# A diagonal of inverse roots in the place of scaled rows, at the norms of a three-layer network

## The chip, the cores and the metric

The kernel runs on one core of a Trainium2 chip. The metric is the device time of one execution in microseconds. The core has five engines that run beside each other, each in its own order, and that wait for one another by semaphores: TensorE (PE; the weight loads of its products are shown as PEld), VectorE (DVE), ScalarE (ACT), GpSimd (POOL) and SyncE (SP), which here issues the loads from memory.

## The reference

256 rows of 1024 f32 numbers go through two layers, each a mixer and an expert feed-forward part, and then through a third block with pooling and attention. Ahead of each of the five parts stands a norm over the rows, and a sixth stands at the end:

```python
def rmsnorm(x, g):
    xf = x.astype(jnp.float32)
    y = xf * lax.rsqrt(jnp.mean(xf * xf, axis=-1, keepdims=True) + RMS_EPS)
    return y.astype(x.dtype) * g

for layer in range(DEPTH):                      # two layers
    x = x + mixer(x, *mixer_params[layer])      # norms 0 and 2
    x = x + peer_ffn(x, *ffn_params[layer])     # norms 1 and 3
...
h = _rmsnorm(x, norm_gain[l])                   # norm 4, ahead of the third block
...
return _rmsnorm(x, final_gain)                  # norm 5
```

Each normed matrix goes into a product with weights at once (`xn @ w_in`, `xi @ w_query`, `h @ w_in[l]`). For such a product the columns of the matrix must lie across the partitions, so it has to be turned.

## The kernel before

`X` holds the 256 rows as two halves of 128 partitions (index `t` or `tt`), each with 1024 f32. Weights come in 680 chunks of 128x1024 through four slots. Each chunk is split on the chip into a high part (`high`, ScalarE, L157) and a low part (`low_v` on VectorE, L162, or `low_g` on GpSimd, L167), and each product with them is three products, high by high, high by low and low by high (L174 to L176, or the two wide ones of L180 and L181). SyncE may load a chunk into a slot when the low part of the chunk four before it is made, and the high part of a chunk is made three chunks ahead of PE. `w_used` counts the chunks that PE is done with.

A norm `n` is spread over four engines, each of which runs its piece in its own order:

- `norm_scalar` (ScalarE): for each half of the rows, the squares of columns 0 to 511 and of 512 to 1023 with their sums (L253), in `SM` columns `2t` and `2t + 1`; then the root (L257) of what VectorE has put into column `4 + t`.
- `norm_sum` and `norm_vector` (VectorE): for each half of the rows, the sum of both columns (L262), the reciprocal of the root (L264), and the scaling of all 1024 columns into the arena tile `xs` (L270). On VectorE this stands behind the four additions to `X` of the part before (`out_add`, L240, ahead of norms 1, 3 and 5; `up_add`, L1261, ahead of norms 2 and 4).
- `norm_tensor` (PE): 8 blocks of 128x128 of each half are turned into the banks 0 to 3 (L285). At norms 1 to 4 idle products of the identity with itself (L275) stand ahead of them: 12 ahead of the first half's blocks and 4 ahead of the second's. Six more follow at the end of every norm. Their result is not used.
- `split_scalar` and `split_vector`: as soon as two blocks of the second half have been turned, ScalarE writes the high part of the turned columns with the gain (L296) and VectorE the low part (L304). PE's first real product of the next stage waits for the low parts of the first two of the eight column blocks (`wait_x`).

Norm 5 has no turning: VectorE multiplies `X` by the reciprocal root and the gain (L2271) and SyncE stores it.

The order on each engine is the order in which the code is written; no scheduler moves anything.

Of the kernel before, what the change touches and what calls it, by code (L numbers as in the profile page):

```python
# [7 lines left out]
ALU = mybir.AluOpType  # L8
ACT = mybir.ActivationFunctionType
# [12 lines left out]
EPS = 1e-6  # L22
# [49 lines left out]
def build(nc, d, out):  # L72
    ctx = ExitStack()
    with ctx:
        def sb(name, shape, dt=F32):
            return ctx.enter_context(nc.sbuf_tensor(name, shape, dt))

        def sem(name):
            return ctx.enter_context(nc.semaphore(name))

        X = sb("X", [128, 2, 1024])
# [24 lines left out]
        SM = sb("sm", [128, 128])  # L106
        PS = ctx.enter_context(nc.psum_tensor("ps", [128, 8, 512], F32))
        scr = nc.dram_tensor("scr_rel", [24, 512], F32, kind="Internal")
        ident = CST[:, C_ID:C_ID + 128]
# [17 lines left out]
        for beside in low_on_g:  # L127
# [8 lines left out]
        n_sq, n_ss, n_sd, n_xs, n_xT, n_xh, n_xl = (sem("norm_" + n) for n in (  # L136
            "squares", "sum", "root", "scaled", "turned", "high", "low"))
# [111 lines left out]
        def norm_scalar(a, n, xs, x_ready):  # L249
            for t in range(2):  # L250
                for h in range(2):
                    x_ready(t, h)
                    a.activation(xs[:, t, h * 512:h * 512 + 512], X[:, t, h * 512:h * 512 + 512], ACT.Square,  # L253
                                 accum_out=SM[:, 2 * t + h:2 * t + h + 1]).then_inc(n_sq, 1)
                a.wait_ge(n_ss, 2 * n + t + 1)
                v = SM[:, 4 + t:5 + t]
                a.activation(v, v, ACT.Sqrt, scale=1.0 / 1024, bias=SM[:, 127:128]).then_inc(n_sd, 1)  # L257

        def norm_sum(v, n, t):
            r = SM[:, 4 + t:5 + t]  # L260
            v.wait_ge(n_sq, 4 * n + 2 * t + 2)
            v.tensor_tensor(r, SM[:, 2 * t:2 * t + 1], SM[:, 2 * t + 1:2 * t + 2], ALU.add).then_inc(n_ss, 1)  # L262
            v.wait_ge(n_sd, 2 * n + t + 1)
            v.reciprocal(r, r).then_inc(vec.sem, vec.up())  # L264
            v.wait_ge(vec.sem, vec.n)

        def norm_vector(v, n, xs):
            for t in range(2):
                norm_sum(v, n, t)
                v.tensor_scalar(xs[:, t, :], X[:, t, :], SM[:, 4 + t:5 + t], None, ALU.mult).then_inc(n_xs, 1)  # L270

        def idle_products(t, bank, count):

            for _ in range(count):
                t.matmul(PS[:, bank, 384:512], ident, ident, start=True, stop=True)  # L275

        def norm_tensor(t, n, xs):
            for tt in range(2):
                if n:
                    idle_products(t, 6 if n % 2 else 3, (12, 4)[tt])  # L280
                t.wait_ge(n_xs, 2 * n + tt + 1)
                for kp in range(4):
                    for j in range(2):
                        k = 2 * kp + j
                        m = t.transpose(PS[:, kp, j * 256 + tt * 128:j * 256 + tt * 128 + 128],  # L285
                                        xs[:, tt, k * 128:k * 128 + 128], ident)
                    if tt == 1:
                        m.then_inc(n_xT, 1)
            idle_products(t, 7, 6)
# [119 lines left out]
        def mixer0_tensor(t):  # L409
            t.wait_ge(cst_in, 16)  # L410
            norm_tensor(t, 0, XS0)

            def q_bank(pair, j):
# [78 lines left out]
        def mixer0_scalar(a):  # L492
            a.wait_ge(eps_up, 1)
            table(a, ACT.Sqrt)
            norm_scalar(a, 0, XS0, lambda t, h: a.wait_ge(x_in[t], 16))
            high(a, 0)
            high(a, 1)
# [77 lines left out]
        def mixer0_vector(v):  # L575
# [5 lines left out]
            v.wait_ge(x_in[0], 16)  # L581
            v.wait_ge(x_in[1], 16)
            norm_vector(v, 0, XS0)
            low_v(v, 0)
            low_v(v, 1)
# [323 lines left out]
        def peer_tensor(t, l):  # L909
            wq, down, up = bases(l)  # L910
            n = 2 * l + 1
            norm_tensor(t, n, XS)

            for c in range(16):
# [123 lines left out]
        def peer_scalar(a, l):  # L1038
            wq, down, up = bases(l)
            n = 2 * l + 1  # L1040
            norm_scalar(a, n, XS, lambda t, h: x_after_out(a, 2 * l, t, h))
            split_scalar(a, n, (PV_FFN0, PV_FFN1)[l])
            for c in range(16):
# [219 lines left out]
        def peer_vector(v, l):  # L1263
            wq, down, up = bases(l)
            n = 2 * l + 1
            norm_vector(v, n, XS)
            split_vector(v, n, (PV_FFN0, PV_FFN1)[l])
            for c in range(16):
# [174 lines left out]

        def mixer1_tensor(t):
            norm_tensor(t, 2, XS)

            def nat_bank(nb, tt):
# [148 lines left out]

        def mixer1_scalar(a):
            norm_scalar(a, 2, XS, lambda t, h: x_after_up(a, 1, t, h))
            split_scalar(a, 2, PV_MIX1)

# [133 lines left out]

        def mixer1_vector(v):
            norm_vector(v, 2, XS)
            split_vector(v, 2, PV_MIX1)

# [432 lines left out]
        def block2_vector(v):  # L2171
# [31 lines left out]
            for c in range(24):  # L2203
# [13 lines left out]
                if c == 16:  # L2217
                    v.wait_ge(sw_up, 1)
                    for g in range(4):
                        m = v.scalar_tensor_tensor(out=MIX[:, g, :], in0=MIX[:, g, :], scalar=PVT[:, PV_PS + g:PV_PS + g + 1],  # L2220
                                                   in1=SAG[:, g, :], op0=ALU.mult, op1=ALU.mult)
# [43 lines left out]
                low_v(v, W0 + c + 2)  # L2265
            out_add(v, 4, W0 + 7, 10)
            for t in range(2):
                norm_sum(v, 5, t)
                if t == 0:
                    v.wait_ge(fg_in, 16)  # L2270
                v.scalar_tensor_tensor(out=X[:, t, :], in0=X[:, t, :], scalar=SM[:, 4 + t:5 + t], in1=FG, op0=ALU.mult,  # L2271
                                       op1=ALU.mult).then_inc(out_up, 1)
# [39 lines left out]
        @block.vector  # L2312
        def _(eng):
            mixer0_vector(eng)
            peer_vector(eng, 0)
            mixer1_vector(eng)
            peer_vector(eng, 1)
            block2_vector(eng)
# [108 lines left out]
```

## Time and profile before

| what | us |
|---|---|
| median of 3 runs | 2176.23 |
| lowest and highest | 2171.87, 2176.41 |
| the profiled execution | 2174.84 |
| its span in the profile | 2173.0 |
| PE busy | 2132.8 |
| VectorE busy | 1467.4 |
| ScalarE busy | 1278.1 |
| GpSimd busy | 349.4 |

The profile is one execution. Its span runs from the first to the last record; the time of the execution is 1.8 us more. Busy time is the sum of an engine's records. Matmuls are pipelined, so their durations overlap, and the pace of a row of them is read from their starts: where a row of the timeline stands for a merged group (`x8`), the start of the next row less its own start, divided by the count, is the time for one. "L285" is line 285 of the kernel. In brackets stands the time that the engine was idle ahead of the row and what ended it.

### The profile page before, as it was taken

What the parts mean: (1) busy time and instruction counts of PE and PEld (TensorE: products, weight loads), DVE (VectorE), ACT (ScalarE), POOL (GpSimd) and SP (SyncE); (2) the same over time, 40 slices, a digit from 0 to 9 for tenths busy, and PEclk for the clock granted to TensorE, in tenths of its full rate; (3) what the DMA queues carried; (4) which work ended last, traced back from release to release, by engine and by line L of the source; (5) the groups of instructions that cost most, each with busy time, mean ns of one, the idle gap of its engine ahead of it and who ended that gap; (6) DMA issues with size and microseconds to landing.
All of it is one profiled execution on the core that took longest, in us unless ns stands there. A gap on an engine that the chain in (4) does not pass through costs nothing.

```text
span 2173.0 us, 32843 instructions
## 1 busy us (share of the span) xinstructions
PE 2132.8 (98%) x12752; PEld 1860.5 (86%) x12752; DVE 1467.4 (68%) x2593; ACT 1278.1 (59%) x2172; POOL 349.4 (16%) x160
## 2 busy tenths in 40 slices
PE   8899999999999999997999999999999999999998
PEld 7789988888888888876899888888888888898997
DVE  7658988889855555557489888898555555423445
ACT  6655488877644444465545788776444444444454
POOL 1437800000000000001378000000000000243131
PEclk9999999999999999999999999999999999999999
DMA  6445655555566666642356555555666666754244
GB/s 219 146 133 165 183 172 171 169 167 172 174 196 193 194 193 194 194 165 91 117 165 185 168 172 174 166 167 163 203 193 193 194 193 194 258 184 146 78 136 126
DMA packets 104317, 373.19 MB, mean 172 GB/s; under 512 B 11564, under 2 KB 15044, under 8 KB 103780
## 3 DMA queue, kind: packets, MB, share of 16 engines
q1 hardware_dynamic: 104164, 371.11, 55.6%
q8 instruction: 101, 1.65, 0.3%
q14 instruction: 52, 0.43, 0.1%
HBM read 369.96 MB, written 1.10 MB: 171 GB/s over the span
## 4 chain that ended last, share of the span: by engine, by line
PE 91%; DVE 4%; ACT 2%; DMA 1%; issue 1%; POOL 0%; SPq 0%; ACTq 0%; DVEq 0%
PE ps L180 20%; PE ps L174 18%; PE ps L175 17%; PE ps L176 17%; PE ps L181 10%; PE ps L905 3%; PE ps L1950 1%; DVE WL L162 1%; PE ps L1928 1%; DMA raw<-in_w_qk_dram 1%; PE ps L275 1%; PE ps L884 1%; PE ps L1936 0%; DVE arena L1686 0%; PE ps L1410 0%
## 5 line engine op out<-in xcount | busy, mean ns | idle before, releaser
L157 ACT ACTIVATE WH<-raw 128x1024 fp32r<-128x1024 f32 x680 | 717.4, 1056 | 499.9 <-PE ps L176 450.9
L162 DVE TENSOR_TENSOR WL<-raw,WH 128x1024 fp32r<-128x1024 f32 x556 | 680.0, 1225 | 102.8 <-ACT WH L157 102.7
L180 PE MATMUL ps<-X,WH 128*128 128x512 f32 x1888 | 668.8, 398 | 0.1
L181 PE MATMUL ps<-X,WL 128*128 128x256 f32 x1888 | 527.9, 280 | 0.0
L167 POOL TENSOR_TENSOR WL<-raw,WH 128x1024 fp32r<-128x1024 f32 x124 | 307.7, 2484 | 1006.2 <-ACT WH L157 1005.3
L180 PEld LDWEIGHTS ps<-X,WH 128*128 128x128 f32 x1888 | 353.9, 187 | 78.9 <-issue 0.5
L174 PE MATMUL ps<-WH,X 128*128 128x512 f32 x960 | 379.7, 396 | 4.8 <-DVE X L733 1.6
L175 PE MATMUL ps<-WL,X 128*128 128x512 f32 x960 | 376.1, 392 | 0.0
L176 PE MATMUL ps<-WH,X 128*128 128x512 f32 x960 | 376.0, 392 | 0.0
L181 PEld LDWEIGHTS ps<-X,WL 128*128 128x128 f32 x1888 | 356.8, 189 | 0.0
L174 PE MATMUL ps<-X,WH 128*128 128x256 f32 x896 | 256.4, 286 | 0.8 <-DVE WL L162 0.6
L175 PE MATMUL ps<-X,WH 128*128 128x256 f32 x896 | 253.7, 283 | 0.0
L176 PE MATMUL ps<-X,WL 128*128 128x256 f32 x896 | 253.7, 283 | 0.0
L174 PEld LDWEIGHTS ps<-WH,X 128*128 128x128 f32 x960 | 181.9, 189 | 45.2 <-DVE X L1594 2.0
L176 PEld LDWEIGHTS ps<-WH,X 128*128 128x128 f32 x960 | 181.5, 189 | 38.3
L175 PEld LDWEIGHTS ps<-WL,X 128*128 128x128 f32 x960 | 181.8, 189 | 37.3 <-issue 0.5
L174 PEld LDWEIGHTS ps<-X,WH 128*128 128x128 f32 x896 | 171.9, 192 | 6.4 <-issue 3.0
L175 PEld LDWEIGHTS ps<-X,WH 128*128 128x128 f32 x896 | 172.0, 192 | 0.1
L176 PEld LDWEIGHTS ps<-X,WL 128*128 128x128 f32 x896 | 171.9, 192 | 0.0
L989 ACT ACTIVATE ONE<-ONE,GATE 128x128 f16<-128x128 f16 x512 | 167.6, 429 | 0.0
L1250 DVE TENSOR_TENSOR X<-arena,X 128x512 fp32r<-128x512 f32 x84 | 58.1, 692 | 161.9 <-ACT X L1036 161.9
L176 PE MATMUL ps<-WH,GL 128*128 128x512 f32 x352 | 137.0, 389 | 0.0
(295 smaller groups left out, 2367.6 us busy)
## 6 DMA issues: line engine op xcount, KB each, us to landing
raw<-in_l_down_dram SPq DMA_DIRECT2D x256, 512.0 KB, 3.6
raw<-in_l_up_dram SPq DMA_DIRECT2D x256, 512.0 KB, 4.2
raw<-in_l_wq_dram SPq DMA_DIRECT2D x32, 512.0 KB, 3.6
raw<-in_w_qk_dram SPq DMA_DIRECT2D x24, 512.0 KB, 3.9
raw<-in_w_gates_dram SPq DMA_DIRECT2D x24, 512.0 KB, 3.6
raw<-in_l_nat_dram SPq DMA_DIRECT2D x16, 512.0 KB, 3.5
raw<-in_l_wout_dram SPq DMA_DIRECT2D x16, 512.0 KB, 3.6
raw<-in_l_win_dram SPq DMA_DIRECT2D x16, 512.0 KB, 3.8
```

What stands on the lines that cost most here:

```text
L157: a.activation(WH[:, i % NW, :], raw[:, i % NW, :], ACT.Copy).then_inc(w_high, 1)
L162: v.tensor_tensor(WL[:, i % NW, :], raw[:, i % NW, :], WH[:, i % NW, :], ALU.subtract).then_inc(w_low_v, 1)
L167: g.tensor_tensor(WL[:, i % NW, :], raw[:, i % NW, :], WH[:, i % NW, :], ALU.subtract).then_inc(w_low_g, 1)
L174: t.matmul(o, a[0], b[0], start=first, stop=False)
L175: t.matmul(o, a[0], b[1], start=False, stop=False)
L176: return t.matmul(o, a[1], b[0], start=False, stop=last)
L180: t.matmul(PS[:, bank, :], w[0], X2[:, k, :, :].rearrange("p w t -> p (w t)"), start=first, stop=False)
L181: return t.matmul(PS[:, bank, 0:256], w[1], X2[:, k, 0, :], start=False, stop=last)
L275: t.matmul(PS[:, bank, 384:512], ident, ident, start=True, stop=True)
L905: m = t.matmul(PS[:, 6 + j // 4, (j % 4) * 128:(j % 4) * 128 + 128], ONE[:, s % 2, 0, g, :, tt], ROWS[:, s % 2, 1 + k, g, :, tt], start=(k ...
L989: a.activation(ROWS[:, s % 2, 1, g, :, t], ROWS[:, s % 2, 2, g, :, t], ACT.Copy, scale=GATE0[:, 8 * s + j:8 * s + j + 1]).then_inc(row_0, 1)
L1250: v.tensor_tensor(gl, G[:, 2 * p:2 * p + 2, :].rearrange("p e t -> p (e t)"), gh, ALU.subtract).then_inc(g_low, 1)
```

## The change

At norms 0 to 4 VectorE no longer scales the 1024 columns. It multiplies the identity matrix by the reciprocal roots of the 128 rows, into the first 128 columns of the same half of `xs` (`diagonal`), and PE makes the product of each unscaled block of `X` with this diagonal matrix, where it transposed the scaled block with the identity before. The products stand where the transposes stood, and the idle products stay.

At all six norms the halves' sums are joined in another way. VectorE takes the first sum alone, divides it by 1024 and adds epsilon, into the new columns 6 and 7 of `SM` (`norm_bias`), and needs only the first of the two squares for that. ScalarE takes the root of the second sum over 1024 with this column as its bias; it now waits for its own second square as well as for VectorE.

No instruction changes its place, and each engine has as many in the program as before. On VectorE a 128x1024 multiplication becomes one of 128x128 ten times, and an addition of 128x1 becomes a multiply-add of 128x1 twelve times.

```diff
@@ norm_scalar
-                a.wait_ge(n_ss, 2 * n + t + 1)
-                v = SM[:, 4 + t:5 + t]
-                a.activation(v, v, ACT.Sqrt, scale=1.0 / 1024, bias=SM[:, 127:128]).then_inc(n_sd, 1)
-
-        def norm_sum(v, n, t):
+                a.wait_ge(n_ss, 2 * n + t + 1)
+                a.wait_ge(n_sq, 4 * n + 2 * t + 2)
+                a.activation(SM[:, 4 + t:5 + t], SM[:, 2 * t + 1:2 * t + 2], ACT.Sqrt, scale=1.0 / 1024,
+                             bias=SM[:, 6 + t:7 + t]).then_inc(n_sd, 1)
+
+        def norm_bias(v, n, t):
+            v.wait_ge(n_sq, 4 * n + 2 * t + 1)
+            v.tensor_scalar(SM[:, 6 + t:7 + t], SM[:, 2 * t:2 * t + 1], 1.0 / 1024, EPS, ALU.mult,
+                            ALU.add).then_inc(n_ss, 1)
+
+        def norm_inverse(v, n, t):
             r = SM[:, 4 + t:5 + t]
-            v.wait_ge(n_sq, 4 * n + 2 * t + 2)
-            v.tensor_tensor(r, SM[:, 2 * t:2 * t + 1], SM[:, 2 * t + 1:2 * t + 2], ALU.add).then_inc(n_ss, 1)
             v.wait_ge(n_sd, 2 * n + t + 1)
             v.reciprocal(r, r).then_inc(vec.sem, vec.up())
             v.wait_ge(vec.sem, vec.n)
 
+        def diagonal(xs, t):
+
+            return xs[:, t, 0:128]
+
         def norm_vector(v, n, xs):
             for t in range(2):
-                norm_sum(v, n, t)
-                v.tensor_scalar(xs[:, t, :], X[:, t, :], SM[:, 4 + t:5 + t], None, ALU.mult).then_inc(n_xs, 1)
+                norm_bias(v, n, t)
+                norm_inverse(v, n, t)
+                v.tensor_scalar(diagonal(xs, t), ident, SM[:, 4 + t:5 + t], None, ALU.mult).then_inc(n_xs, 1)
@@ norm_tensor
-                        m = t.transpose(PS[:, kp, j * 256 + tt * 128:j * 256 + tt * 128 + 128],
-                                        xs[:, tt, k * 128:k * 128 + 128], ident)
+                        m = t.matmul(PS[:, kp, j * 256 + tt * 128:j * 256 + tt * 128 + 128],
+                                     X[:, tt, k * 128:k * 128 + 128], diagonal(xs, tt), start=True, stop=True)
@@ block2_vector, norm 5
-                norm_sum(v, 5, t)
+                norm_bias(v, 5, t)
+                norm_inverse(v, 5, t)
```

## Rows read from the trace of the kernel before

**Rows 1.** The page: span, PE's busy time, and the chain's share by engine.
```profile
span 2173.0 us, 32843 instructions
...
PE 91%; DVE 4%; ACT 2%; DMA 1%; issue 1%; POOL 0%; SPq 0%; ACTq 0%; DVEq 0%
```

**Rows 2.** Timeline, weight loads at norm 4: start us, us, engine, line, operation, tiles, count.
```profile
1865.27 2.87 PEld L275 LDWEIGHTS ps<-cst 128*128 128x128 f32 x24
1868.06 0.91 PEld L285 LDWEIGHTS ps<-cst,arena 128*128 128x128 f32 x8
1868.94 0.97 PEld L275 LDWEIGHTS ps<-cst 128*128 128x128 f32 x8
1869.83 0.91 PEld L285 LDWEIGHTS ps<-cst,arena 128*128 128x128 f32 x8
1870.70 1.42 PEld L275 LDWEIGHTS ps<-cst 128*128 128x128 f32 x12
1872.22 0.19 PEld L174 LDWEIGHTS ps<-WH,X 128*128 128x128 f32 x1
```

**Rows 3.** Timeline, VectorE and ScalarE at norm 4.
```profile
1865.59 0.18 ACT L253 ACTIVATION_READ_ACCUMULATOR arena<-X 128x1 f32 x1
1865.69 0.69 DVE L1261 TENSOR_TENSOR X<-X,ps 128x512 f32<-128x512 f32 x1
1866.30 0.15 DVE L262 TENSOR_TENSOR sm<-sm 128x1 f32<-128x1 f32 x1
...
1867.01 0.75 DVE L270 TENSOR_SCALAR arena<-X,sm 128x1024 f32<-128x1024 f32 x1
...
1868.76 0.75 DVE L270 TENSOR_SCALAR arena<-X,sm 128x1024 f32<-128x1024 f32 x1
...
1870.36 3.03 ACT L296 ACTIVATE X<-ps,pvt 128x256 fp32r<-128x256 f32 x8 [1.83 <-PE ps L285]
...
1871.23 0.87 DVE L304 SCALAR_TENSOR_TENSOR X<-ps,pvt,X 128x256 fp32r<-128x256 f32 x2 [1.72 <-ACT X L296]
```

**Rows 4.** Timeline, weight loads: first idle and first real product of norm 1.
```profile
137.30 2.87 PEld L275 LDWEIGHTS ps<-cst 128*128 128x128 f32 x24
...
144.25 0.19 PEld L180 LDWEIGHTS ps<-X,WH 128*128 128x128 f32 x1
```

**Rows 5.** Records of single lines: count, then shortest, median and longest in ns.
```profile
L275 PE MATMUL ps<-cst x188: 269/275/276, 12.4 to 1872.0; 128*128 128x128 f32 x188
...
L285 PE MATMUL ps<-cst,arena x80: 272/273/447, 9.2 to 1870.7; 128*128 128x128 f32 x80
...
L884 PE MATMUL ps<-arena x128: 269/275/276, 152.7 to 1126.8; 128*128 128x128 f32 x128
```

**Rows 6.** Groups on VectorE, shapes apart: count, busy us, mean ns, idle before.
```profile
L1732 DVE TENSOR_SCALAR arena<-ps,sm 128x128 f32<-128x128 f32 x8 | 2.4, 347 | 0.3 <-PE ps L1434 0.2
...
L264 DVE RECIPROCAL sm<-sm 128x1 f32<-128x1 f32 x12 | 2.0, 164 | 4.3 <-ACT sm L257 4.3
```

**Rows 7.** Timeline behind norm 4: ScalarE and the weight loads.
```profile
1881.37 1.06 ACT L157 ACTIVATE WH<-raw 128x1024 fp32r<-128x1024 f32 x1 [7.03 <-DMA raw<-in_w_qk_dram]
...
1882.78 0.19 PEld L176 LDWEIGHTS ps<-WH,X 128*128 128x128 f32 x1
1883.74 0.19 PEld L174 LDWEIGHTS ps<-X,WH 128*128 128x128 f32 x1 [0.77 <-DVE WL L162]
```

**Rows 8.** Timeline, weight loads at norm 0 and at the third chunk behind it.
```profile
9.14 3.15 PEld L285 LDWEIGHTS ps<-cst,arena 128*128 128x128 f32 x16 [9.14 <-issue]
12.26 1.42 PEld L275 LDWEIGHTS ps<-cst 128*128 128x128 f32 x12
14.03 0.19 PEld L174 LDWEIGHTS ps<-X,WH 128*128 128x128 f32 x1 [0.35 <-issue]
...
20.34 0.19 PEld L174 LDWEIGHTS ps<-X,WH 128*128 128x128 f32 x1 [0.51 <-DVE WL L162]
```

**Rows 9.** Timeline, VectorE at norm 5.
```profile
2167.99 0.15 DVE L262 TENSOR_TENSOR sm<-sm 128x1 f32<-128x1 f32 x1
```

## Prediction

> **What bounds the kernel now.** I read the page first. TensorE is busy for 98% of the span [rows 1], and the chain that ended last lies on PE for 91% of it [rows 1]. Time that is added to TensorE's own stream is therefore added to the kernel, unless PE later waits for something that does not depend on it. So the question at each norm is what TensorE waits for there, and the timeline of one norm answers it. I took norm 4, the one ahead of block 2, and looked at the weight loads, because each record of a product has one and their starts show the pace of the stream.
>
> At norm 4 the stream is almost unbroken [rows 2]: 24 records of idle products from 1865.27, 8 transposes from 1868.06, 8 records of idle products from 1868.94, 8 transposes from 1869.83, 12 records of idle products from 1870.70, and the first real product of the stage at 1872.22. That is 6.95 us. VectorE and ScalarE run beside it. The first half of the rows is scaled by 1867.01 + 0.75 = 1867.76, which is 0.3 us before PE reaches its transposes; the second half by 1868.76 + 0.75 = 1869.51, 0.3 us before PE gets to it [rows 3]. So neither scaling is what PE waits for: what stands ahead of each group of transposes is the fixed number of idle products. At the end the two lines nearly meet. The last group of idle products is issued out at 1870.70 + 12 x 0.111 = 1872.03 (0.111 is 8 records in 1869.83 - 1868.94), and the low parts of the first two column blocks are ready at 1871.23 + 0.87 = 1872.1 [rows 3]. PE goes on at 1872.22, some 0.15 us after its own stream would have let it. Norm 1 has the same stretch, 137.30 to 144.25, or 6.95 us [rows 4], and so have norms 2 and 3, one like the other.
>
> **What one product costs against one transpose.** This is the term that matters, and the trace holds both. The 94 idle products of the program (6 at norm 0, 22 at each of norms 1 to 4) leave 188 records; the 80 transposes leave 80 [rows 5]. A full product of two f32 operands is thus two passes, each with a weight load; a transpose is one. It is no property of the identity matrix, since the products with the sub-keys in the expert layers are 128 records for the 64 products of both layers [rows 5]. Passes of either kind follow each other at the same pace: 8 of the idle products in 0.89 us, 8 transposes in 0.88 or 0.87 [rows 2], so 0.11 us a pass. A product in the place of a transpose costs 0.11 us more of PE.
>
> The Trainium skill (TensorE: Matmul & The Clock Gate, Terms) calls the transpose mode four times faster for FP32. By that the 16 products of a norm would cost 16 x 3 x 0.11 = 5.3 us more and not 1.8. The records disagree with it here, since there are two passes for each product and not four; it comes back as a rival.
>
> **Norms 1 to 4, part by part.** *On PE:* 16 transposes become 16 products, so 16 more passes of 0.111, +1.78 us. *The scaling:* 128x1024 (0.75) becomes 128x128. The trace has no such instruction between two on-chip tiles on VectorE; the bounds are the reciprocal of 128x1, 0.16, and the 128x128 scaling out of the product banks, 0.35 [rows 6]. I take 0.25, nearer to the middle, and it does not matter: each group already sits behind idle products that end 0.3 us later than the scaling did, and the gain of 0.5 only makes that slack larger. *The sum of the halves:* the addition on VectorE, 0.15, becomes a multiply-add of the same 128x1. For the first half of the rows it still stands behind the four additions to X in VectorE's own order (it starts at 1866.30 when the fourth, started at 1865.69 and 0.69 long, is ending [rows 3]), although the squares were done at 1865.59 + 0.18 = 1865.8. So the root of the first half starts no earlier. For the second half the new order lets the root start right after the squares, about 0.2 us sooner; together with the smaller scaling the diagonal is there some 0.7 us sooner, and again PE is not there yet. *The new waits:* the root also waits for ScalarE's own squares, behind which nothing but the next squares is queued. Zero.
>
> Then what is late at the end of the norm? PE's stream would end at 1872.03 + 1.78 = 1873.8. The other chain: the second group starts 0.89 later (the 8 extra passes of the first group), its first two blocks take 4 passes and not 2 (+0.22), so ScalarE's first split starts at 1870.36 + 1.11 = 1871.5, VectorE's first at 1872.3, and PE could go on at 1871.5 + 1.86 = 1873.3 (1.86 is 1872.22 - 1870.36 [rows 2, 3]). PE's own stream is last, and the 0.15 us that it waited before is used up. So a norm costs 1.78 - 0.15, about **1.65 us**, between 1.6 (pace 0.109) and 1.9 (pace 0.118 and no wait used up).
>
> Is it given back? In the expert layers PE is never let wait by weights, so norms 1 and 3 keep theirs. Behind norm 2 PE waits for VectorE and ScalarE work that is made of PE's own earlier output, so that moves along. Behind norm 4 there is one wait that does not depend on PE: ScalarE sits 7.0 us for a weight transfer that lands at 1881.37, and PE waits for the parts of that chunk [rows 7]: its load would have been due at 1882.78 + 0.23 = 1883.0 and came at 1883.74, 0.7 later, of which the product then under way covered 0.2. The transfer had been issued before the norm, so a PE that comes 1.65 us later finds the chunk ready and wins 0.5 us back. Sum: 3 x 1.65 + (1.65 - 0.5) = **+6.1 us**.
>
> **Norm 0.** Here PE does wait for the scaling: it has no idle products ahead, and starts at 9.14 [rows 8], right after the scaling of the first half. With a diagonal it starts about 0.5 us sooner, at 8.6. Its first passes are slow, though: 16 transposes from 9.14 to 12.26, 0.195 each on the mean, and (14.03 - 12.26) / 12 = 0.15 at most from then on [rows 8], against 0.11 at norm 4. I read that as the lower of the two levels, 1.2 GHz, for most of the transposes, and the higher after it. Now 32 passes are to be made. If the higher level comes between 11.5 and 12.1, about 14 to 16 passes are done by then, and the other 16 to 18 at 0.11 end at 13.5 to 13.9. Twelve idle passes end at 14.8 to 15.2, against 14.03 for the first real product before. Of that the next wait takes back a part: at 20.34 PE had waited 0.5 us for the third chunk [rows 8], whose chain runs over VectorE's split of this norm (which starts when both other weights' low parts are done and the split on ScalarE has begun, now about 0.4 us later). I take **+0.6 us**, between -0.2 (the chain over VectorE decides, and gains) and +1.3 (nothing is taken back).
>
> **Norm 5** has no products. Its multiply-add stands where the addition stood, behind the last addition to X for the first half and, for the second, behind the output's first scaling, at 2167.99 [rows 9], so the roots start as before. Zero, within 0.05.
>
> **Sum:** 6.1 + 0.6 + 0 = +6.7 us. The profiled execution took 2174.84 us, of which 2173.0 are its span [rows 1] and 1.8 lie around it, and would come to 2181.5; against the median of 2176.23, 1.4 above it, that is **2182.9 us**, or 0.31% slower.
>
> **The rivals.**
> *A product costs no more than a transpose* (one pass where one operand is a diagonal with data, or the second pass hidden): then PE's stream stays as it is at norms 1 to 4, and only norm 0 gains about 0.2 us: 2176.0. Against it stand the pass counts of rows 5. 9%.
> *The data's way decides, not PE's stream:* if the idle products were really waiting room, PE would wait for the scaling, and the shorter scaling and the earlier second root would give 0.5 + 0.2 us at each of five norms, against the 0.22 us of the first two blocks: -2.4 us, 2173.8. It decides from the point where PE stands idle ahead of the transposes at norms 1 to 4, and rows 2 show it busy there. 4%.
> *More is given back:* PE comes later to chunks whose low parts GpSimd makes, and to the attention's waits; if each norm gets back half, the sum is 3 to 4 us: 2179.7. 9%.
> *Four passes in all,* the page's factor: 16 x 3 x 0.11 = 5.3 us at norms 1 to 4, less 0.65, and some 2.5 at norm 0: 2199. 3%. The forecast has 75%.
>
> **How the numbers follow.** The forecast's own bounds are 3 x 1.6 + 1.0 - 0.2 = 5.6 and 3 x 1.9 + 1.4 + 1.3 = 8.4 us: 2181.8 to 2184.6. Runs of the same kernel lay between 2171.87 and 2176.41, so a median of a few may be 2 us off. The range reaches down to the case in which more is given back: 2178.0 to 2187.0. A difference under 0.2% (4.4 us) can't be told from none. Of the forecast's 75%, some 6 fall below that line by scatter; with the 3 of the four passes that makes slower 0.72. Faster takes 2 of the data's way and 2 of the cheap product by scatter, 0.04. The rest, 6 + 9 + 2 + 7, is same, 0.24.
>
> **What would show it.** In the profile of the changed kernel: the line of the new products has 160 PE records with starts 0.11 us apart, not 80; from the first idle record of norms 1 to 4 to the first real product 8.6 us and not 6.95; PE without a wait for the diagonal there; the wait at 1883.74 gone; scaling near 0.25 us on VectorE. It is wrong if the records are 80, or if the stretch stays 6.95, or if PE's waits behind the norms shrink by more than 0.5 us in sum.

## The result and the profile after

| | us |
|---|---|
| changed kernel, median of 10 runs | 2180.78 (2179.42 to 2182.42) |
| kernel before, median of 10 runs beside them | 2175.43 (2171.87 to 2177.21) |
| ratio, with its 95% interval | 1.0027 (1.0019 to 1.0036) |
| span of the profiled execution, before and after | 2173.0 and 2179.6 |

The change makes the kernel slower by 0.27%, some 5.9 us (4.1 to 7.8 by the interval). The page of the changed kernel has 80 more records on PE than that of before, and VectorE is busy for 4.6 us less (1462.8 against 1467.4):

```profile
span 2179.6 us, 33015 instructions
PE 2141.8 (98%) x12832; PEld 1868.8 (86%) x12832; DVE 1462.8 (67%) x2593; ACT 1278.3 (59%) x2172; POOL 349.4 (16%) x160
```

The weight loads at norm 4 in the changed kernel, whose lines are now L285 for the idle products and L295 for the products with the diagonal; they answer [rows 2]:

```profile
1870.82 2.87 PEld L285 LDWEIGHTS ps<-cst 128*128 128x128 f32 x24
1873.61 1.87 PEld L295 LDWEIGHTS ps<-arena,X 128*128 128x128 f32 x16
1875.39 0.97 PEld L285 LDWEIGHTS ps<-cst 128*128 128x128 f32 x8
1876.29 1.87 PEld L295 LDWEIGHTS ps<-arena,X 128*128 128x128 f32 x16
1878.07 1.42 PEld L285 LDWEIGHTS ps<-cst 128*128 128x128 f32 x12
1879.41 0.19 PEld L174 LDWEIGHTS ps<-WH,X 128*128 128x128 f32 x1
```

The stretch from the first idle pass to the first real product is 1879.41 - 1870.82 = 8.59 us where it was 6.95. The same stretch is 8.60 at norms 1 to 3. Each group of 8 blocks is 16 passes in 1.78 us where it was 8 in 0.88. The count of the line's records answers [rows 5], and the new scaling [rows 6]:

```profile
L295 PE MATMUL ps<-arena,X x160: 274/275/551, 8.6 to 1878.1; 128*128 128x128 f32 x160
...
L280 DVE TENSOR_SCALAR arena<-cst,sm x10: 285/288/289, 8.2 to 1874.2; 128x128 f32<-128x128 f32 x10
```

VectorE in the changed kernel at norm 4, against [rows 3]: the second diagonal is ready at 1874.16 + 0.29 = 1874.45, and PE comes to it at 1876.29. It lies there for 1.8 us, where the scaled rows lay ready for 0.3.

```profile
1872.55 0.29 DVE L280 TENSOR_SCALAR arena<-cst,sm 128x128 f32<-128x128 f32 x1
...
1874.16 0.29 DVE L280 TENSOR_SCALAR arena<-cst,sm 128x128 f32<-128x128 f32 x1
...
1877.91 2.83 DVE L314 SCALAR_TENSOR_TENSOR X<-ps,pvt,X 128x256 fp32r<-128x256 f32 x7 [3.46 <-ACT X L306]
```

At norm 0 (against [rows 8]) PE starts sooner, at 8.61, and is later at the end: the first real product stands at 15.15 and not 14.03. At the third chunk behind it, which PE had waited 0.51 us for, no wait is left; the load that stood at 20.34 stands at 20.89.

```profile
8.61 5.29 PEld L295 LDWEIGHTS ps<-arena,X 128*128 128x128 f32 x32 [8.61 <-issue]
13.81 1.42 PEld L285 LDWEIGHTS ps<-cst 128*128 128x128 f32 x12
15.15 0.19 PEld L174 LDWEIGHTS ps<-X,WH 128*128 128x128 f32 x1
...
20.89 0.19 PEld L174 LDWEIGHTS ps<-X,WH 128*128 128x128 f32 x1
```

Behind norm 4 (against [rows 7]) the wait of 0.77 on the weight loads is gone too, though ScalarE still sits 6.4 us for the transfer:

```profile
1887.43 1.06 ACT L157 ACTIVATE WH<-raw 128x1024 fp32r<-128x1024 f32 x1 [6.42 <-DMA raw<-in_w_qk_dram]
```
```profile
1889.97 0.19 PEld L176 LDWEIGHTS ps<-WH,X 128*128 128x128 f32 x1
1890.20 0.19 PEld L174 LDWEIGHTS ps<-X,WH 128*128 128x128 f32 x1
```

**Where the 6.6 us of the two profiles lie.** I cut both spans at the norms: the start of each norm's first idle pass, and the first real product behind it. The norms 1 to 4 take 4 x 1.65 = 6.6 us more. Between them, the first mixer from the start of the span to norm 1 is 1.0 shorter (137.30 and 136.29), the first expert part is 2.2 longer, the second mixer 0.6 shorter, the second expert part the same within 0.1, and the last stretch 0.6 shorter (300.81 and 300.17). The sum is 6.6. The 2.2 us were in no term of mine: the same code and the same waits, in a part of the program that the change does not touch. The second profiles below tell what they are, and that the 1.0 us of the first mixer are a shift of the granted clock, less what norm 0 costs.

### The profile page after: what moved, and what is told of

It is laid out like the page before. It is cut to its first block, busy times and chain, and to the rows that moved or that the text cites. A ratio compares the mean times of both kernels' runs of the same rounds, so it can differ in the third digit from the quotient of the medians.

```text
span 2179.6 us, 33015 instructions
## 1 busy us (share of the span) xinstructions
PE 2141.8 (98%) x12832; PEld 1868.8 (86%) x12832; DVE 1462.8 (67%) x2593; ACT 1278.3 (59%) x2172; POOL 349.4 (16%) x160
## 4 chain that ended last, share of the span: by engine, by line
PE 93%; DVE 3%; ACT 2%; issue 1%; POOL 0%; DMA 0%; SPq 0%; ACTq 0%; DVEq 0%
PE ps L180 20%; PE ps L174 18%; PE ps L175 18%; PE ps L176 18%; PE ps L181 10%; PE ps L915 3%; PE ps L1960 1%; PE ps L285 1%; PE ps L1938 1%; PE ps L295 1%; DVE WL L162 1%; PE ps L894 1%; PE ps L1946 0%; DVE arena L1696 0%; PE ps L1420 0%
## 5 line engine op out<-in xcount | busy, mean ns | idle before, releaser
L174 PE MATMUL ps<-WH,GH 128*128 128x512 f32 x352 | 137.1, 389 | 0.0
```

Source lines behind the costliest of these rows:

```text
L174: t.matmul(o, a[0], b[0], start=first, stop=False)
```

## Experiments

Every ratio is that to the kernel before, timed beside it on the same chip. "Stretch" is the time from the first idle pass to the first real product at each of norms 1 to 4, read as above.

**1. The bias alone.** The changed kernel with the scaling of all columns and the transposes of before.

```diff
-                v.tensor_scalar(diagonal(xs, t), ident, SM[:, 4 + t:5 + t], None, ALU.mult).then_inc(n_xs, 1)
+                v.tensor_scalar(xs[:, t, :], X[:, t, :], SM[:, 4 + t:5 + t], None, ALU.mult).then_inc(n_xs, 1)
...
-                        m = t.matmul(PS[:, kp, j * 256 + tt * 128:j * 256 + tt * 128 + 128],
-                                     X[:, tt, k * 128:k * 128 + 128], diagonal(xs, tt), start=True, stop=True)
+                        m = t.transpose(PS[:, kp, j * 256 + tt * 128:j * 256 + tt * 128 + 128],
+                                        xs[:, tt, k * 128:k * 128 + 128], ident)
```

> Of the change only the joining of the two sums by the root's bias is made; the rows are scaled and transposed as before. Theory: it lies beside TensorE's stream at norms 1 to 4, so the stretch from the first idle pass to the first real product stays 6.95 us and the time is that of before, ratio 0.9995 to 1.0005. Rival (the way of the data decides): the root of the second half starts 0.2 us sooner at each of five norms, 1 us or 0.05% less, and the stretch shrinks.

Measured: ratio 0.9996 (0.9987 to 1.0005), stretch 6.95 at all four. The joining of the sums by the bias is worth nothing that this measurement can tell, as the theory had it. The time alone would also fit the rival's 0.05%; the stretch does not:

```profile
1862.23 2.87 PEld L285 LDWEIGHTS ps<-cst 128*128 128x128 f32 x24
...
1869.18 0.19 PEld L174 LDWEIGHTS ps<-WH,X 128*128 128x128 f32 x1
```

**2. Products of scaled rows with the identity.** The kernel before, with one line changed.

```diff
-                        m = t.transpose(PS[:, kp, j * 256 + tt * 128:j * 256 + tt * 128 + 128],
-                                        xs[:, tt, k * 128:k * 128 + 128], ident)
+                        m = t.matmul(PS[:, kp, j * 256 + tt * 128:j * 256 + tt * 128 + 128],
+                                     xs[:, tt, k * 128:k * 128 + 128], ident, start=True, stop=True)
```

> The rows are scaled as before, all 1024 columns, but turned by a full product with the identity and not by a transpose. Theory: the second pass of each product is the whole price; the stretch at norms 1 to 4 is 8.5 to 8.6 us as with the diagonal, and the time is that of the changed kernel within 0.05%, ratio to before 1.0025 to 1.0035. Rival (the diagonal itself, being made or read, costs something): this one is clearly faster than the changed kernel.

Measured: 1.0025 (1.0016 to 1.0034), stretch 8.60. That is the changed kernel's time and its stretch, without a diagonal and without a shorter scaling. So the 0.47 us that each scaling saves on VectorE buys nothing, and what costs is that a product takes the place of a transpose.

**3. The diagonal alone,** with the sum and the constant bias of before.

```diff
-                v.tensor_scalar(xs[:, t, :], X[:, t, :], SM[:, 4 + t:5 + t], None, ALU.mult).then_inc(n_xs, 1)
+                v.tensor_scalar(xs[:, t, 0:128], ident, SM[:, 4 + t:5 + t], None, ALU.mult).then_inc(n_xs, 1)
...
-                        m = t.transpose(PS[:, kp, j * 256 + tt * 128:j * 256 + tt * 128 + 128],
-                                        xs[:, tt, k * 128:k * 128 + 128], ident)
+                        m = t.matmul(PS[:, kp, j * 256 + tt * 128:j * 256 + tt * 128 + 128],
+                                     X[:, tt, k * 128:k * 128 + 128], xs[:, tt, 0:128], start=True, stop=True)
```

> The diagonal and its products, but with the sum of the halves on VectorE and the root's constant bias as before. Theory: as the changed kernel, ratio 1.0025 to 1.0035, stretch 8.5 to 8.6 us. Rival: the late root of the second half, 0.2 us later at each norm, shows as +1 us over the changed kernel.

Measured: 1.0025 (1.0016 to 1.0034), stretch 8.60. The rival, 1 us over the changed kernel, would be 1.0032, which the interval still holds; the stretches tell more sharply that nothing is lost by the later root.

**4. As many passes by idle products.** The kernel before, with nothing of the change, and 8 more idle products at each of norms 1 to 4.

```diff
-                    idle_products(t, 6 if n % 2 else 3, (12, 4)[tt])
+                    idle_products(t, 6 if n % 2 else 3, (12, 8)[tt])
...
-            idle_products(t, 7, 6)
+            idle_products(t, 7, 10 if n else 6)
```

> The kernel before, with transposes, and 8 more idle products (16 passes) at each of norms 1 to 4: 12, 8 and 10 for 12, 4 and 6. Nothing of the change is in it. Theory: TensorE's stream is the whole price, so the stretch is 8.6 us as in the changed kernel and the ratio to before is 1.0022 to 1.0032, less by the 0.6 us of norm 0. Rival (the product or the diagonal has a price beside its passes): clearly faster than the changed kernel, ratio under 1.002.

Measured: 1.0029 (1.0018 to 1.0040), stretch 8.56. Sixteen passes that compute nothing cost what the change costs. This is the cleanest evidence for the cause, as no data, no VectorE work and no operand differ from the kernel before. The rows of norm 4:

```profile
1871.34 2.87 PEld L275 LDWEIGHTS ps<-cst 128*128 128x128 f32 x24
1874.13 0.91 PEld L285 LDWEIGHTS ps<-cst,arena 128*128 128x128 f32 x8
1875.01 1.86 PEld L275 LDWEIGHTS ps<-cst 128*128 128x128 f32 x16
1876.79 0.91 PEld L285 LDWEIGHTS ps<-cst,arena 128*128 128x128 f32 x8
1877.66 2.31 PEld L275 LDWEIGHTS ps<-cst 128*128 128x128 f32 x20
1879.90 0.19 PEld L174 LDWEIGHTS ps<-WH,X 128*128 128x128 f32 x1
```

**5. The changed kernel with fewer idle products.** If the stream of PE decides, then the idle products can be cut down to where the diagonal is just ready.

```diff
-                    idle_products(t, 6 if n % 2 else 3, (12, 4)[tt])
+                    idle_products(t, 6 if n % 2 else 3, (9, 0)[tt])
...
-            idle_products(t, 7, 6)
+            idle_products(t, 7, 3 if n else 6)
```

> The changed kernel with fewer idle products at norms 1 to 4: 9 ahead of the first half's blocks, none ahead of the second's, 3 behind (12, 4 and 6 before). Theory: TensorE's stream is what decides, and the diagonal is ready long before it; with 20 passes fewer the stretch is 8.55 - 2.1 = 6.45 us, 0.5 less than the 6.95 of before, and the time is 2 us under before, ratio 0.999, and 8 us under the changed kernel, 0.9965. Rival: the idle products were needed for the clock or cover other waits, and what is cut comes back as waiting: no gain over the changed kernel.

Measured: 0.9997 (0.9988 to 1.0006), 2174.57 us, which is 6.2 under the 2180.78 of the changed kernel (timed on another occasion), where 8 were expected. The stretch is 6.53 where 6.45 was expected, 0.42 less than before. The granted clock was at its higher level at all four norms. The expected 2 us under the kernel before can't be seen in the median, 0.3 us under, though the interval still holds them. Two things stand against them in the profile, which is of the slowest of the eleven executions. PE comes out of norm 0 late (its first real product stands at 15.88), and behind norm 4 the wait is longer:

```profile
1866.48 2.20 PEld L285 LDWEIGHTS ps<-cst 128*128 128x128 f32 x18
1868.61 3.65 PEld L295 LDWEIGHTS ps<-arena,X 128*128 128x128 f32 x32
1872.18 0.75 PEld L285 LDWEIGHTS ps<-cst 128*128 128x128 f32 x6
1873.02 0.19 PEld L174 LDWEIGHTS ps<-WH,X 128*128 128x128 f32 x1
...
1885.67 0.19 PEld L174 LDWEIGHTS ps<-X,WH 128*128 128x128 f32 x1 [1.91 <-DVE WL L162]
```

PE waits 1.91 us on its weight loads for the chunk that it waited 0.77 for in the kernel before and not at all in the changed one. From norm 4's end (the first real product behind it) to the end of the span it is 301.95 us, against 300.81 and 300.17.

The kernel before was not trimmed in the same way, so this doesn't show that the diagonal is needed for the 0.42 us. Its scaled rows lay ready 0.3 us before PE took them [rows 2, 3]; by an estimate from these rows some 0.3 of the 0.42 us could be had with transposes too.

**6. The same, with scaling and transposes at norm 0.** The edit of experiment 5, and:

```diff
-                v.tensor_scalar(diagonal(xs, t), ident, SM[:, 4 + t:5 + t], None, ALU.mult).then_inc(n_xs, 1)
+                o, i_ = (diagonal(xs, t), ident) if n else (xs[:, t, :], X[:, t, :])
+                v.tensor_scalar(o, i_, SM[:, 4 + t:5 + t], None, ALU.mult).then_inc(n_xs, 1)
...
-                        m = t.matmul(PS[:, kp, j * 256 + tt * 128:j * 256 + tt * 128 + 128],
-                                     X[:, tt, k * 128:k * 128 + 128], diagonal(xs, tt), start=True, stop=True)
+                        o = PS[:, kp, j * 256 + tt * 128:j * 256 + tt * 128 + 128]
+                        m = (t.matmul(o, X[:, tt, k * 128:k * 128 + 128], diagonal(xs, tt), start=True, stop=True)
+                             if n else t.transpose(o, xs[:, tt, k * 128:k * 128 + 128], ident))
```

> The changed kernel with 9, 0 and 3 idle products at norms 1 to 4, and at norm 0 the scaling and the transposes of before, with the new bias. Theory: norm 0 gives back 0.6 us, norms 1 to 3 are 0.42 us each shorter than in the kernel before, and norm 4's gain goes into the wait for the weight transfer behind it: 1.3 us under before, ratio 0.9994. Rival: norm 0's 0.6 us are absorbed later in the first mixer, and it stands at the trimmed kernel's 0.9997.

Measured: 1.0011 (1.0003 to 1.0020). Both expectations failed; it is slower than the kernel before. The stretch is 6.53 again, so the loss lies elsewhere. In its profile the wait behind norm 4 has grown to 3.83 us, and the stretch from there to the end to 305.3. That profile is of the slowest of the twelve executions (2180.61 us, where the median is 2176.54), so it shows where such an execution loses, and not how much the median one does:

```profile
1885.70 1.06 ACT L157 ACTIVATE WH<-raw 128x1024 fp32r<-128x1024 f32 x1 [10.10 <-DMA raw<-in_w_qk_dram]
```
```profile
1888.07 0.29 PEld L174 LDWEIGHTS ps<-X,WH 128*128 128x128 f32 x1 [3.83 <-DVE WL L162]
1888.23 0.33 PEld L175 LDWEIGHTS ps<-X,WH 128*128 128x128 f32 x1
1888.45 0.33 PEld L176 LDWEIGHTS ps<-X,WL 128*128 128x128 f32 x1
```

The spacing of the loads behind it, 0.16 and 0.22 us where the same loads stand 0.10 and 0.12 apart in the kernel before, goes with a granted clock that is at the lower of its two levels from there (0.51 of full speed between 1888.0 and 1891.4); the weight loads had just stood still for 3.8 us. In nine of the ten profiles in which the table is loaded first, ScalarE could take the chunk 16.1 to 16.8 us after norm 4 began, whatever the norm's length; in this one it was 18.7. The nine had issued the chunk 3.6 us before norm 4 began and it landed 19.7 to 20.4 us later; here it was issued 2.9 us before and took 21.7. Why both were so is open.

**7. The table out of the way.** The chunk behind norm 4 stands in the queue behind a table of 4608 KB (`scr_rel`, issued just before it), which takes 19 us to land. In this experiment the table goes in 8 pieces between later chunks.

```diff
             s.wait_ge(rel_out, 16)
-            s.dma_start(SK, bass.AP(scr, 0, [[1, 128], [512, 24], [1, 384]])).then_inc(sk_in, 16)
             for i in range(B2 + 4, G0 + 19):
                 load(s, i)
+                p, r = divmod(i - B2 - 8, 2)
+                if r == 0 and 0 <= p < 8:
+                    s.dma_start(SK[:, 3 * p:3 * p + 3, :], bass.AP(scr, 1536 * p, [[1, 128], [512, 3], [1, 384]])
+                                ).then_inc(sk_in, 16)
...
-                    v.wait_ge(sk_in, 16)
+                    v.wait_ge(sk_in, 128)
```

In the kernel before:

> The kernel before, but the 4.6 MB table that is loaded in front of the third block's first weight chunks goes in 8 pieces between later chunks, one behind every second chunk. Theory: the chunk behind norm 4 lands early, TensorE's wait for it (0.6 to 1.2 us in the two profiles of before) is gone, the stretch from norm 4's end to the end of the span falls from 300.8 and 301.4 to about 300.2, and the time by 0.6 to 1.2 us, ratio 0.9996. Rival: the pieces delay later chunks and a new wait stands there.

In the changed kernel:

> The changed kernel with the table in the same 8 pieces. Theory: it did not wait for that chunk any more, so its stretch from norm 4's end to the end stays at 300.1 to 300.2, as against before_late's equal value: then norm 4 costs its full 1.65 us, where the wait behind it gave back 0.6 in the changed kernel as timed. Rival (the wait gave nothing back): after_late is shorter by the same amount as before_late.

In the kernel of experiment 6:

> Diagonal products with 9, 0 and 3 idle products at norms 1 to 4, scaling and transposes at norm 0, and the table in the same 8 pieces. Theory: what was lost in trim_not_at_0 was the wait for the chunk behind norm 4 (3.8 us on the weight loads, 305.3 us from norm 4 to the end); with it gone that stretch is 300.2, each norm 1 to 4 is 6.53, and the time is 4 x 0.42 + 0.6 to 1.2 = 2.3 to 2.9 us under before, ratio 0.9988. Rival: a shorter norm loses the clock or another wait, and the stretch stays over 301.

From norm 4's end to the end of the span, each kernel with and without the edit:

| | table first | table in pieces |
|---|---|---|
| kernel before | 300.81, 301.40 (two profiles) | 300.18 |
| changed kernel | 300.17, 300.12 (two profiles) | 300.11 |
| trimmed, transposes at norm 0 | 305.31 | 300.13 |

This is as the theory had it, to 0.1 us. In the changed kernel the transfer cost nothing any more, in the kernel before it cost 0.6 to 1.2 us, and a shorter norm 4 runs into it. So part of the change's price at norm 4 was given back by that wait. The other kernels with the table first agree: 300.77 with the stretch of before (experiment 1), 300.14 to 300.19 with a stretch of 8.56 or 8.60 (experiments 2 to 4). In time, the kernel before is not measurably faster by the edit (1.0000, 0.9990 to 1.0009), as 0.6 us of 2175 are too little to see. The trimmed kernel with the table in pieces has the lowest median of all, 2172.51 us: 0.9992 of before (0.9983 to 1.0001). The expected 0.9988 lies within the interval, and so does no difference. Against experiment 6, 1.0003 to 1.0020 without this edit, the intervals do not overlap, so in time too the trimmed kernel lost something by the table in front. Its profile at norm 4:

```profile
1864.04 2.20 PEld L286 LDWEIGHTS ps<-cst 128*128 128x128 f32 x18
1866.16 3.65 PEld L297 LDWEIGHTS ps<-arena,X 128*128 128x128 f32 x32
1869.73 0.75 PEld L286 LDWEIGHTS ps<-cst 128*128 128x128 f32 x6
1870.57 0.19 PEld L174 LDWEIGHTS ps<-WH,X 128*128 128x128 f32 x1
```

The changed kernel with the table in pieces had a span of 2182.1 in its one profile, 2.5 us over the first profile of the changed kernel. Norms and the last stretch are the same within 0.1; the difference is in the first mixer (norm 1 begins at 139.18 and not 136.29), which the edit does not touch.

**8. Second profiles of both kernels.** What of the other stretches belongs to a kernel, and what to an execution?

> The kernel before, unchanged, for a second profile. The expert layers' stretches (between the first real product behind norms 1 and 3 and the first idle pass of norms 2 and 4) were 790.6 or 793.0 us in the profiles so far. If that is the execution's and not the kernel's, this profile shows another draw, each stretch at one of the two values; if it is the kernel's, the first layer is 790.6 and the second 793.1 again.

> The changed kernel, unchanged, for a second profile. Norms 1 to 4 are 8.60 us again, by the theory. Whether the expert layers are at 790.6 or 793.0, and whether the first mixer takes 121.1 us or more, tells if these are draws of the execution; if they are the kernel's, it shows 792.8, 793.1 and 121.1 again.

The kernel before, second profile: first real product behind norm 1 and first idle pass of norm 2, then the same of norms 3 and 4.

```profile
144.81 0.19 PEld L180 LDWEIGHTS ps<-X,WH 128*128 128x128 f32 x1
...
937.88 0.19 PEld L275 LDWEIGHTS ps<-cst 128*128 128x128 f32 x1
...
1074.50 0.19 PEld L180 LDWEIGHTS ps<-X,WH 128*128 128x128 f32 x1
...
1865.04 0.19 PEld L275 LDWEIGHTS ps<-cst 128*128 128x128 f32 x1
```

| expert part, us | first | second |
|---|---|---|
| before, first profile | 790.6 | 793.1 |
| before, second profile | 793.1 | 790.5 |
| changed, first profile | 792.8 | 793.1 |
| changed, second profile | 793.1 | 790.6 |

The same code takes one time or the other. In all 13 profiles, 26 expert parts, 5 took 790.5 to 790.6 and 21 took 792.8 to 793.1; nothing lay between. It is a draw of the execution, worth 2.2 to 2.5 us each time, so the 2.2 us of the first part are not the change's. In the shorter ones the wide passes follow each other evenly at 0.23 us, in the longer ones a share of them at 0.24. What draws the one or the other is open.

The second mixer took 121.95 to 123.47 us over the 13 profiles, 123.47 and 122.73 in the two of the kernel before, 122.84 and 122.03 in the two of the changed one. Its 0.6 us are within that scatter, and whether the change has a share in them is open.

The first mixer has a draw too. For 3.4 us the granted clock is at its lower level there, around 87 us in one first profile and 77 in the other. The kernel before, then the changed one, in two windows of 6 us (PE busy, granted clock, share of the DMA engines, GB/s):

```profile
76.00:82.00 6.00, 5.91 (x35) 1.00 0.15 42
86.00:92.00 6.00, 4.53 (x17) 0.72 0.34 123
```
```profile
76.00:82.00 6.00, 6.00 (x29) 0.72 0.12 31
86.00:92.00 6.00, 3.97 (x23) 1.00 0.43 156
```

At 77 us the loss goes into a wait for GpSimd that follows, which is 2.33 us and not 3.58; at 87 it comes behind that wait and is not covered. The two waits for GpSimd on either side of 77 us, in the kernel before and in the changed one:

```profile
74.22 1.19 PE L395 MATMUL ps<-arena 128*128 128x64 f32 x9 [1.05 <-POOL arena L772]
...
87.47 0.77 PE L397 MATMUL ps<-arena 128*128 128x128 f32 x2 [3.58 <-POOL arena L772]
```
```profile
74.78 0.63 PE L405 MATMUL ps<-arena 128*128 128x64 f32 x4 [1.03 <-POOL arena L782]
...
88.03 0.80 PE L407 MATMUL ps<-arena 128*128 128x128 f32 x5 [2.33 <-POOL arena L782]
```

From the first of them to norm 1 it is 63.1 us in the kernel before and 61.5 in the changed one. In the first pair of profiles this made norm 1 begin 1.0 us sooner in the changed kernel, though it was 0.6 us late at 74 us. In its second profile the low stretch lies at 87.6 and norm 1 begins at 137.52, against 137.30 and 137.86 for the kernel before.

The rows at 74 us stand ahead of this draw and show what norm 0 costs. Over all 13 profiles PE is there at 73.87 to 74.34 us where norm 0 has transposes (seven) and at 74.42 to 76.00 where it has products (six), 1.0 us later on the mean. The times with products scatter by 1.6 us for two reasons. The first pass starts at 7.5 to 8.8 us. And PE goes from 0.21 to 0.11 us a pass, together with the granted clock, at a time that differs by the execution: 12.1 us in the first profiles of both kernels, up to 14.7 in others. In the changed kernel with the table in pieces it was 14.7, with the same code at norm 0:

```profile
8.48 6.58 PEld L295 LDWEIGHTS ps<-arena,X 128*128 128x128 f32 x32 [8.48 <-issue]
14.99 1.42 PEld L285 LDWEIGHTS ps<-cst 128*128 128x128 f32 x12
16.33 0.19 PEld L174 LDWEIGHTS ps<-X,WH 128*128 128x128 f32 x1
```

## Why the prediction was right, and where not

- *PE's stream at norms 1 to 4, +1.65 us each.* Right to the digit: 8.60 for 6.95, in all five profiles with the products and the full count of idle products. The reasons hold one by one: two passes for a product, 0.11 us a pass, and a wait of 0.15 us before the first real product that was used up. Experiments 2 and 4 show that the passes are the cause.
- *VectorE's savings are worth nothing.* Right, by experiments 1 and 2 in time and by 3 in the stretches. The new scaling took 0.29 us where I took 0.25.
- *Norm 4 gives back 0.5 us.* Right in kind, 0.6 by the last stretch (300.81 and 300.17), 1.2 against the second profile of before. Experiment 7 shows the wait by taking away what made it.
- *Norm 0, +0.6.* Right in kind; that the one profile hit the foreseen times is luck. The first real product was foreseen at 14.8 to 15.2 and stood at 15.15; over the six profiles with products at norm 0 it stood at 14.76 to 16.33. I had taken the rise of the clock for fixed, between 11.5 and 12.1 us, from a single profile; it came between 12.1 and 14.7. By PE's wait at 74 us the price is 0.6 us in the first pair and 1.0 on the mean, within my -0.2 to +1.3. The take-back at the third chunk is a part of that: the wait of 0.5 us is gone.
- *Norm 5, nothing.* Right within 0.1: the last stretch is 300.18 with the old sum (kernel before, table in pieces) and 300.11 with the new.
- *The sum,* +6.7 for a measured +5.9 (4.1 to 7.8 by the interval). The medians of 10 runs differ by 5.4, just under my own bounds of 5.6 to 8.4, and 2180.78 us lies under their 2181.8; the wider range, drawn down to 2178.0 for the case that more is given back, holds it. Of the 2.1 us between forecast and median, 0.8 are the starting point: I added to a median of 3 runs, 2176.23, and that of 10 is 2175.43. The spans of the first pair differ by 6.6, and that this is so near to 6.7 is luck: 2.2 more in the expert part are nearly cancelled by 1.6 less by the clock in the first mixer and 0.6 less in the second. I made nothing of the draws in the expert parts. They don't change the expected time if both kernels draw them equally often, which 13 profiles can't tell; but two profiles may differ by 5 us through them alone, and a reader of this single pair would have put 2.2 us down to the change.
- *The rivals.* That a product costs as much as a transpose, and that it costs four passes, fall with 160 records for 80 products. That the data's way decides falls with experiment 2. That half is given back, which left 3 to 4 us, falls less sharply: it lies just below the interval of 4.1 to 7.8. In the profiles only the wait behind norm 4 gives back, 0.6 to 1.2 us, while the expert parts behind norms 1 and 3 take the same two values in both kernels; behind norm 2 the scatter hides what there may be.
- *The factor of four* of the Trainium skill (TensorE: Matmul & The Clock Gate, Terms) is not what this f32 case shows: 1.78 us for 8 products against 0.88 for 8 transposes is a factor of two.

## What to carry to other kernels

Turning by a product with a diagonal matrix saves a scaling on VectorE but costs a second pass for each f32 block on TensorE; it can pay only where PE waits for the scaling, and for longer than the added passes take. At norm 0 PE does wait for it, and the products cost 1.0 us there all the same. First read from the weight loads whether PE really waits. Where it is kept busy with idle products, count those in too, since with the diagonal ready sooner some of them can go (in experiment 5, 10 of 22 at a norm, which won back 6 us). A stage that is made shorter can run into the next transfer, here one queued behind a table of 4608 KB, and what was gained is lost there unless the transfer is moved as well.

## What the runs showed of the hardware that I had not expected

The same code, with the same waits, takes 790.5 or 793.0 us (792.8 to 793.1) in an expert part, by the execution. Ahead of norm 3 the lower level of the granted clock came for 3.4 or 6.8 us at a time in stretches where PE waits between short pieces of work (1.0 and 3.6 us for GpSimd at 74 and 87 us of the kernel before), and at other moments in each execution (once between 77 and 90 us in 11 of 13 profiles, and two or three times between 987 and 1039). At norm 0 of the kernel before, by the spacing of the passes in [rows 8], PE went from the lower level to the higher at 12.1 us, while it had made nothing but transposes since its first record. In the six other profiles with transposes at norm 0 it rose at 13.0 to 14.2 us, when the idle products had begun at 11.9 to 12.6.
